# Hybrid decoder layer on one Trainium2 core: bias products and first weight loads moved into the normalisation's block, key/value eviction placed ahead of the exponentials

## The reference, cut to what matters

```python
h = _rms_norm(x, p['norm_pre_mix'][l])
proj = h @ p['w_in'][l]
a_qkv, b_qkv, z, b_pre, a_pre, gate_a, gate_b = jnp.split(proj, SPLIT_IDX, axis=-1)
a_qkv = a_qkv.reshape(Bsz, L, N_GROUPS, 3, H_G, HD_A)
...
# GROUPS = ((128, 1), (512, 4), (2048, 16)); per group g, keys at distances 0, d, 2d, ...
biases.append(rel_bias[bucket][:, g * H_G:(g + 1) * H_G].T.astype(jnp.float32))
s = (jnp.einsum('bqhd,bqjhd->bhqj', qg, kv_sel[:, :, :, 0]).astype(jnp.float32) * ATTN_SCALE
     + biases[g][None, :, None, :])
m = jnp.max(s, axis=-1, keepdims=True)
p = jnp.exp(s - m)
...
beta = jax.nn.sigmoid(b_pre.astype(jnp.float32))
g = -jnp.exp(p['a_log'][l].astype(jnp.float32)) * jax.nn.softplus(
    a_pre.astype(jnp.float32) + p['dt_bias'][l].astype(jnp.float32))
```

## Time and profile before

| | us |
|---|---|
| median of 3 runs (2455.25 to 2456.33) | 2455.29 |
| the profiled execution's own time | 2455.94 |
| its span in the trace | 2454.2 |
| TensorE busy in the span | 2260.9 (92%) |
| VectorE / ScalarE busy | 1240.2 (51%) / 724.6 (30%) |

### The profile page before, as it was taken

The page is one execution under the profiler, slowest core; times in us unless marked ns, Lnnn a source line. Parts: engine busy times, 40 slices in busy tenths (PEclk is TensorE's granted clock), DMA queues, the critical chain, the costliest instruction groups (busy, mean ns, idle before and its releaser), DMA issues. The chain is left out here.

```text
span 2454.2 us, 36492 instructions
## 1 busy us (share of the span) xinstructions
PE 2260.9 (92%) x14592; PEld 2103.0 (86%) x14592; DVE 1240.2 (51%) x2361; ACT 724.6 (30%) x1620; POOL 65.2 (3%) x76
## 2 busy tenths in 40 slices
PE   5888898699999999999999698897999999889898
PEld 3677787599999999999999698676999999868676
DVE  4123221365676666667666633446666666531243
ACT  4123231323234232332423300454222222231221
POOL 0000000001001010100101000000000000000000
PEclk9989999688999999999999899898999999989999
DMA  4010201441122121312213243521222222151432
GB/s 142 32 65 12 85 12 51 92 104 52 57 58 59 52 83 28 87 58 57 69 46 108 85 134 125 184 87 52 79 82 80 77 77 77 46 171 25 146 116 65
DMA packets 213984, 191.20 MB, mean 78 GB/s; under 512 B 33539, under 2 KB 187172, under 8 KB 213830
## 3 DMA queue, kind: packets, MB, share of 16 engines
q1 hardware_dynamic: 199802, 142.13, 20.0%
q10 hardware_dynamic: 11120, 36.96, 3.8%
q0 software_dynamic: 2944, 10.49, 1.6%
HBM read 138.09 MB, written 51.64 MB: 77 GB/s over the span
## 5 line engine op out<-in xcount | busy, mean ns | idle before, releaser
L265 PE MATMUL bank<-xT_hi,w_lo 128*128 128x344 f32 x1152 | 395.7, 343 | 4.9 <-DVE w_lo L261 4.9
L267 PE MATMUL bank<-xT_hi,w_hi 128*128 128x344 f32 x1152 | 370.0, 321 | 0.0
L266 PE MATMUL bank<-xT_lo,w_hi 128*128 128x344 f32 x1152 | 369.9, 321 | 0.0
L265 PEld LDWEIGHTS bank<-xT_hi,w_lo 128*128 128x128 f32 x1152 | 219.4, 190 | 6.1 <-DVE w_lo L261 5.4
L266 PEld LDWEIGHTS bank<-xT_lo,w_hi 128*128 128x128 f32 x1152 | 219.3, 190 | 0.0
L267 PEld LDWEIGHTS bank<-xT_hi,w_hi 128*128 128x128 f32 x1152 | 218.2, 189 | 0.0
L1093 PE MATMUL bank<-xT_hi,f_hi 128*128 128x258 f32 x704 | 199.6, 283 | 0.0
L1089 PE MATMUL bank<-xT_hi,f_lo 128*128 128x258 f32 x704 | 199.3, 283 | 0.0
L1091 PE MATMUL bank<-xT_lo,f_hi 128*128 128x258 f32 x704 | 199.2, 283 | 0.0
L265 PE MATMUL bank<-fo_wh,fo_sl 128*128 128x512 f32 (+1 forms) x396 | 157.8, 398 | 27.9 <-DVE fo_wl L261 22.9
L266 PE MATMUL bank<-fo_wl,fo_sh 128*128 128x512 f32 (+1 forms) x396 | 156.9, 396 | 0.0
(11 more groups left out here) (407 smaller groups left out, 4947.6 us busy)
## 6 DMA issues: line engine op xcount, KB each, us to landing
w_raw<-in_w_in SPq DMA_DIRECT2D x48, 512.0 KB, 3.9
f_raw<-in_w_ffn_in SPq DMA_DIRECT2D x44, 512.0 KB, 4.9
act_scr<-f_y ACTq DMA_DIRECT2D x22, 516.0 KB, 2.7
fo_sr<-act_scr SPq DMA_DIRECT2D x16, 704.0 KB, 6.7
fo_wr<-in_w_ffn_out SPq DMA_DIRECT2D x22, 512.0 KB, 5.1
gate_scr<-gate ACTq DMA_DIRECT2D x16, 516.0 KB, 3.1
a_kv_raw<-in_w_in SPq DMA_DIRECT2D x3, 2048.0 KB, 9.4
mix_ta<-gate_scr SPq DMA_DIRECT2D x8, 516.0 KB, 4.9
```

The source lines that it names most:

```text
L265: nc.tensor.matmul(out, stat_lo, mov_hi, start=start, stop=False)
L266: nc.tensor.matmul(out, stat_hi, mov_lo, start=False, stop=False)
L267: return nc.tensor.matmul(out, stat_hi, mov_hi, start=False, stop=stop)
```

## The change

Three things are edited. First, the blocks of the normalisation and of the ones are merged into one that also holds the twelve bias products and copies (two a tile, behind the transposes of tiles 0 to 5, in banks 4 to 7), the split of the beta weights, and, at the end of the load queue, the first key/value weights (now in two halves) and query weights. Its loop is written out. The bias tables and the identity are loaded by ScalarE's queue, the first rows ahead of the norm weights. Second, in the attention's block TensorE begins with the beta projection at once, and the first key/value weights are split in halves, ahead of the eviction of the beta projection. Third, in `tile` ScalarE's `fill.slot(t)` (the key/value eviction) stands ahead of `split_q` and `exps`, and VectorE's `split_q` stands behind its `fill.slot(t)`.

```diff
+            def tiles(eng, stage, finish, beside):
+                def at(t):
+                    return eng, t // 2, t % 2, P if t < NT else NS, t
+                stage(*at(0))
+                for t in range(1, NT + 2):
+                    if t <= NT:
+                        stage(*at(t))
+                    finish(*at(t - 1))
+                    beside(t - 1)
...
+                def _(sp):
+                    load(sp, 0, 0, P, 0)
+                    sp.dma_start(wrow[:], weight.partition_broadcast(P)).then_inc(const, 16)
+                    for t in range(1, NT + 1):
+                        load(sp, t // 2, t % 2, P if t < NT else NS, t)
+                        if t == BETA - 2:
+                            loads_beside(sp)
+                    loads_last(sp)
...
+                def _(v):
+                    def beside(t):
+                        for n in (2 * t, 2 * t + 1):
+                            if n < NG * HA:
+                                bias_copies(v, n)
+                        if t == BETA:
+                            beta_dve(v)
...
+            def products(pe, n):
+                if n == 0:
+                    pe.wait_ge(spread, 1)
+                if n >= 4:
+                    pe.wait_ge(cp, n - 3)
+                nc.tensor.matmul(banks[4 + n % 4][:, :3 * P], wide[:, n], onehot[:, n // HA],
+                                 start=True, stop=True).then_inc(mm, 1)
...
+                def first_loads(sp):
+                    for half, loaded in ((slice(0, 4), kv_first), (slice(4, KT), kv_ld)):
+                        sp.dma_start(kv_raw[:, half], w_in[:, half, Q:Q + KV]).then_inc(loaded, 16)
+                    sp.dma_start(q_raw[:], w_in[:, :, :Q]).then_inc(q_ld, 16)
...
-                    bias_load(sp)
-                    beta_load(sp)
-                    load(0, "kv"); load(0, "q")
...
-                    bias_products(pe)
-                    bias_over(pe, False)
                     beta_pe(pe)
                     groups(pe, kv_steps, beta_rest, q_part, tile, 0)
...
                     def tile(g, t, fill):
+                        fill.slot(t)
                         if t == SPLIT_Q and g + 1 < NG:
                             split_q(g + 1)
                         if g != AHEAD and t + 1 < NT:
                             exps(g, t + 1)
-                        fill.slot(t)
...
+                    act.wait_ge(kv_first, 16)
+                    nc.scalar.activation(kv_hi[:, :4], kv_raw[:, :4], ACT.Copy).then_inc(kv_half, 1)
+                    act.wait_ge(kv_ld, 16)
+                    inc(nc.scalar.activation(kv_hi[:, 4:], kv_raw[:, 4:], ACT.Copy), "kv_hi")
                     beta_act(act)
-                    split_kv(0)
                     groups(act, kv_steps, beta_rest, q_part, tile, 1)
...
                     def tile(g, t, fill):
-                        if t == SPLIT_Q + 1 and g + 1 < NG:
-                            split_q(g + 1)
...
                         fill.slot(t)
+                        if t == SPLIT_Q + 1 and g + 1 < NG:
+                            split_q(g + 1)
```

More of the change, by code:

```diff
@@ L129, in build @@
         banks = [pb(ctx, f"bank{i}") for i in range(8)]
[L131 to L239, removed]
@@ new lines, in build, with norm_buffers, norm_block, nothing @@
+        stat = sb(early, "stat", [P, 2, 4])
+        def norm_buffers(s):
+            rows = [sb(s, f"rows{j}", [P, D]) for j in range(2)]
+            normed = [sb(s, f"normed{j}", [P, D]) for j in range(2)]
+            return rows, normed, sb(s, "sq", [P, D]), sb(s, "wrow", [P, D])
+        def norm_block(row_tile, weight, memory, loads_first, loads_beside, loads_last, bias_wide, bias_products, bias_copies,
+                       beta_act, beta_dve):
+            rows, normed, sq, wrow = memory
+            loaded = [ev("loaded"), ev("loaded")]
+            const, squared = sem("const"), [ev("squared", 3, -1), ev("squared", 3, -1)]
+            made = [ev("made", 1, -1), ev("made", 1, -1)]
+            turned = [ev("turned", 2, -1), ev("turned", 2, -1)]
+            hi_done = [ev("hi", 2), ev("hi", 2)]
+            lo_done = [ev("lo", 2, -1), ev("lo", 2, -1)]
+            eps, ones_set, ident_ld = sem("eps"), sem("ones_set"), sem("ident_ld")
+            BETA = 6
+            def tiles(eng, stage, finish, beside):
[7 more added lines that the diff above has]
+                    beside(t - 1)
+            def nothing(*_):
+                pass
+            def nothing(*_):
+                pass
+            def load(sp, i, j, n, t):
+                sp.wait_ge(made[j].sem, made[j].at(i, 0))
+                sp.dma_start(rows[j][:n], row_tile(t)).then_inc(loaded[j].sem, 16)
+            def stats(act, i, j, n, t):
+                act.wait_ge(loaded[j].sem, i * 16 + 16)
+                if j == 0:
+                    act.wait_ge(squared[1].sem, squared[1].at(i, 0))
+                else:
+                    act.wait_ge(squared[0].sem, squared[0].at(i, 3))
+                nc.scalar.activation(sq[:n], rows[j][:n], ACT.Square,
+                                     accum_out=stat[:n, j, 0:1]).then_inc(squared[j].sem, 1)
+                act.wait_ge(squared[j].sem, squared[j].at(i, 1))
+                nc.scalar.activation(stat[:n, j, 1:2], stat[:n, j, 0:1], ACT.Ln, scale=1.0 / D,
+                                     bias=stat[:n, 0, 3:4]).then_inc(squared[j].sem, 1)
+                act.wait_ge(squared[j].sem, squared[j].at(i, 2))
+                nc.scalar.activation(stat[:n, j, 2:3], stat[:n, j, 1:2], ACT.Exp,
+                                     scale=-0.5).then_inc(squared[j].sem, 1)
+            def split_hi(act, i, j, n, t):
+                for half in range(2):
+                    act.wait_ge(turned[j].sem, turned[j].at(i, half + 1))
+                    src = banks[2 * j + half][:].rearrange("p (k c) -> p k c", k=4)[:, :, :n]
+                    nc.scalar.activation(
+                        xT_hi[:, 4 * half:4 * half + 4, bass.ds(t * P, n)], src,
+                        ACT.Copy).then_inc(hi_done[j].sem, 1)
+            def center(v, i, j, n, t):
+                v.wait_ge(squared[j].sem, squared[j].at(i, 3))
+                v.wait_ge(turned[j].sem, turned[j].at(i, 0))
+                nc.vector.scalar_tensor_tensor(normed[j][:n], rows[j][:n], stat[:n, j, 2:3],
+                                               wrow[:n], ALU.mult, ALU.mult).then_inc(made[j].sem, 1)
+            def split(v, i, j, n, t):
+                for half in range(2):
+                    v.wait_ge(hi_done[j].sem, hi_done[j].at(i, half + 1))
+                    src = banks[2 * j + half][:].rearrange("p (k c) -> p k c", k=4)[:, :, :n]
+                    at = (slice(None), slice(4 * half, 4 * half + 4), bass.ds(t * P, n))
+                    nc.vector.tensor_tensor(xT_lo[at], src, xT_hi[at].bitcast(FP),
+                                            ALU.subtract).then_inc(lo_done[j].sem, 1)
+            def turn(pe, i, j, n, t):
+                pe.wait_ge(made[j].sem, made[j].at(i))
+                for half in range(2):
+                    pe.wait_ge(lo_done[j].sem, lo_done[j].at(i, half - 1) if half else lo_done[j].at(i, 0))
+                    for k in range(4):
+                        last = nc.tensor.transpose(banks[2 * j + half][:, k * P:k * P + n],
+                                                   normed[j][:n, (4 * half + k) * P:(4 * half + k + 1) * P],
+                                                   ident[:n, :n])
+                    last.then_inc(turned[j].sem, 1)
+            with nc.Block() as block:
+                @block.sync
+                def _(sp):
[6 more added lines that the diff above has]
+                    loads_last(sp)
+                @block.vector
+                def _(v):
[5 more added lines that the diff above has]
+                            beta_dve(v)
+                    start(v, 1, *(e.sem for e in made + lo_done))
+                    nc.vector.memset(stat[:, :, 3:4], EPS).then_inc(eps, 1)
+                    nc.vector.memset(ident_ones[:], 1.0).then_inc(ones_set, 1)
+                    bias_wide(v)
+                    v.wait_ge(const, 16)
+                    tiles(v, center, split, beside)
+                    v.wait_ge(ones_set, 1)
+                @block.scalar
+                def _(act):
+                    nc.scalar.preload_act_table_set("natural_log_exp_and_others")
+                    def beside(t):
+                        if t == BETA:
+                            beta_act(act)
+                    start(act, 1, *(e.sem for e in squared))
+                    act.dma_start(ident[:], a["c_ident"]).then_inc(ident_ld, 16)
+                    loads_first(act)
+                    act.wait_ge(eps, 1)
+                    tiles(act, stats, split_hi, beside)
+                @block.tensor
+                def _(pe):
+                    def beside(t):
+                        for n in (2 * t, 2 * t + 1):
+                            if n < NG * HA:
```

(66 more changed lines are left out.)

17 lines of the change are left out of this document (9 added, 8 removed).

## The result

The changed kernel takes 2395.61 us (median of 4 runs, 2393.97 to 2398.56) against 2455.27 us: a ratio of 0.9758 with a 95% interval of 0.9741 to 0.9775, 59.7 us faster. The forecast was 2399 us. The profiled execution took 2393.97 us, its span 2392.2 us, 62.0 us less than before's.

What follows compares the result with a forecast made beforehand. TensorE was taken as the bound, with idle and slow-clock stretches at the start and in the query tiles. Gains of 26.1 and 30.2 us, together 56.3, from 2455.94 gave 2399.6, less 0.65 for the median: 2399 us, range 2389 to 2414.

Steps and rivals of the forecast that it cites:

- The chain of the sum: Start: normalisation ends at 44.3, beta projection at 58.1, key/value pass follows directly, 23.3 us earlier; 26.1 with the faster clock.
- the restart's 2.8 us: First key/value passes: without an idle stretch ahead, 14 slow passes run at the upper clock level, gaining 2.8 us.
- the longer normalisation: Normalisation, tiles 0 to 5: two products make PE the bound at 4.59 us a tile against 3.48; +6.5 us, end at 44.3.
- The rival, in which each pair adds its full 2.62 (2408 us): Normalisation: no product time hides, so it ends at 53.6 us and the kernel takes 2408 us; chance 0.08.
- The forecast case, products at the lower level: Normalisation: PE's clock stays low, a bias product keeps 1.31 us, and the kernel takes 2399 us; chance 0.60.
- the rival (2393 us): Normalisation: the clock rises, products at half price fit the pace, the block ends near 38.3; 2393 us, chance 0.17.
- The cover: Start: key/value weights are split by 52.1 us, 6 us before the beta projection ends at 58.1, so PE does not wait.
- all eight waits: Query tiles: PE's 8 waits for the key/value eviction `a_kv`, 21.1 us together, all go.
- 30.2 in the sum: Tiles 3 to 6: gain of 16.5 us in group 0 and 13.7 in group 1, waits 21.1 plus slow stretches 9.1.
- the reference: Tile 2 of groups 0 and 1, 11.19 and 10.56 us, used as the tile length without a wait to size the gain.
- Exponentials one eviction later: Query tiles: exponentials behind an eviction (0.57 us) cost nothing, as ScalarE idles there; uncovered with the query split, 10.4 us.
- the next wait: Query tiles, rival: PE waits for ScalarE instead, 10.4 us stretched by the slow clock to 14.9; 2414 us, chance 0.10.

Runs made afterwards that it cites:

- start_only: The changed kernel with the order of ScalarE and VectorE in the query tiles set back; 2431.48 us, a ratio of 0.9896.
- one_a_tile: The changed kernel with one bias product a tile in tiles 0 to 7, four in group 0's key/value tiles, bias table widened after the first scaling; 2389.68 us.
- full_rows: The changed kernel with the factors of the bias products padded with zeros from 33 to 128 rows; 2388.05 us, a ratio of 0.9731.
- loads_late: The changed kernel with the first key/value and query weights loaded at the beginning of the attention's block instead of the normalisation's end; 2393.62 us.
- order_only: The kernel before with only the change's new order in the query tiles; 2421.88 us, a ratio of 0.9869.
- order_scalar_only: The changed kernel with VectorE's query split put back at the head of tile 5, ScalarE keeping its new order; 2393.77 us, a ratio of 0.9752.

## Why the prediction was right, point by point

**The start.** The chain of the sum held: one run of products out of the way, no gap between the beta projection and the key/value tiles, no slow restart. With the restart's 2.8 us counted in, the first query pass comes 146.55 − 122.94 = 23.6 us earlier, where the sum had 26.1, and start_only gives 24.1. The term that was off is the longer normalisation: +6.5 was taken, 46.89 − 37.84 = 9.05 was measured. Two parts make up most of the difference. A tile took 4.76 and not 4.59, since a product between transposes costs some 1.43 and not 1.31: 6 × 0.17 = 1.0. And the first transposes came late, at 11.08 against 9.92 before, though the first rows were worked on earlier (4.76 against 6.69): VectorE idled 7.41 us for the table `onehot`, and the scaling of the first tile stood behind the widening of the bias table in VectorE's queue. The sum had no term for that; it had even taken some tenths off for the early rows. one_a_tile, which scales first, shows its price: its transposes start 3.2 us earlier. The rival, in which each pair adds its full 2.62 (2408 us), did not happen.

**The clock in the normalisation.** The forecast case, products at the lower level, was right, and the rival (2393 us) that comes nearest to the measured time was wrong in its mechanism, for no product ran at the upper level. The Trainium skill's page "TensorE: Matmul & The Clock Gate" (Part 1: The HAM clock gate) says that sustained activity lifts the clock. PE was busy without a gap from 20 to 40 us in the changed kernel, and yet its transposes stayed at 1.97 us: being busy was not enough there, and the measurement decides. In full_rows the clock rose as the page says. What the rival got right is the price: with the clock up the products hide completely.

**The loads.** The cover was there as predicted: weights split at 54.90, needed at 60.62. loads_late shows that nearly all of this margin was not needed.

**The tiles.** The mechanism held, and all eight waits went. The size was 30.2 in the sum and 33.7 in order_only. What was mis-sized is the reference: tile 2 of groups 0 and 1, which I took as tiles without a wait, shrank too, from 11.19 to 10.87 and from 10.56 to 291.73 − 281.79 = 9.94. In start_only they take 11.19 and 10.56 again, so the difference is caused by the same order. In group 1 the trace of before has one of the eight waits in that tile, of 0.3 us, so it was no tile without a wait; the list names none in tile 2 of group 0. Exponentials one eviction later, and VectorE's split at its new place, cost nothing, as costed. ScalarE did not become the next wait.

**How near the number came.** The start gave 2.5 us less than its term and the tiles 3.5 more, and these two errors partly cancel. That 2399 lies only 3.4 us from the measured 2395.61 is in part luck; the mechanism does not hang on it.

**What stays open.** The profiled spans differ by 62.0 us and the medians by 59.7. Of the 62.0, 403.31 − 345.10 = 58.2 had been gained when group 2's query passes began; the other 3.8 lie behind that point. From there to the end of the span the ten profiles take between 2046.0 and 2052.0 us (before 2050.9, the changed kernel 2047.1), and kernels with the same code there lie at both ends: loads_late 2046.8, order_scalar_only 2050.2. So the 3.8 us are no more than what single executions scatter; what makes them scatter is not shown.

## What to carry to other kernels

An in-order engine's program is a queue with a price: look for work whose input is long ready and that stands behind work that must wait, and move it ahead; here that gave 33.7 us for two moved steps, of which one, the eviction on ScalarE, was enough. When a wait on the busiest engine goes, count the slow stretch behind it as well, and take the reference from a place that the same wait can't touch. Before work is moved into another engine's idle time, compare its length there with the pace of that stretch: two products a tile did not fit, one did.

## What the runs showed of the hardware that I had not expected

- Products of 33 rows left PE at its lower level however closely they stood; the same products with 128 rows, most of them zeros, brought the normalisation to the upper level, with 1.46 instead of 2.93 us a pair. Padding a small contraction made the kernel 7.6 us faster.
- The granted clock's column can't be relied on at the start of the span: the window from 20 to 30 us of the changed kernel and of full_rows reads 1.00 in both, while a tile's transposes take 1.97 us in the one and 1.09 in the other.

The window of the changed kernel, then that of full_rows:

```profile
20.00:30.00 10.00, 10.00 (x25) 5.46 (x24) 7.23 (x10) 5.46 (x13) 0.00 (x0) 1.00 0.52 150
```

```profile
20.00:30.00 10.00, 7.16 (x36) 4.52 (x36) 9.81 (x16) 7.70 (x18) 0.00 (x0) 1.00 0.60 171
```

- A fp32 product of 33 rows and 384 columns in a running stream of passes cost some 1.05 us at the upper level (one_a_tile, granted clock 1.00 around it), more than half of its 1.43 at the lower one (the changed kernel).
